# Mixture-of-experts outputs: one accumulating row pair per token in memory in place of eight separate rows per token

## The reference, cut to what matters

```
scores = sigmoid(h @ router_w)                  # 64 experts, 8 groups; each token gets 8 experts of 4 groups
gates  = 2.5 * scores of the chosen 8 / their sum
y      = sum over the 8 chosen e of (silu(h @ we_gate[e]) * (h @ we_up[e]) * gate_e) @ we_down[e]
shared = (silu(h @ ws_gate) * (h @ ws_up)) @ ws_down
x      = LN(alpha * x + (1 + gate2) * (y + shared))
```

## Time and profile before

| what | us |
|---|---|
| runs | 1685.2, 1704.44, 1702.05 (median 1702.05) |
| the profiled execution, by its own time | 1687.51 |
| its span, from the first to the last instruction | 1685.8 |
| TensorE busy | 1433.9 (85%) |
| VectorE busy | 581.6 (35%) |
| POOL busy | 243.8 (14%) |
| DMA moved | 318.40 MB, mean 189 GB/s |

### The profile page before, as it was taken

One profiled execution on the slowest core, in us unless ns is written; L12 is line 12 of the kernel. 1 busy time (PEld: TensorE's weight loads), 2 busy tenths in 40 slices (PEclk: granted clock), 3 DMA queues, 4 the chain that ended last, 5 costly groups with the idle time before them and its releaser, 6 DMA issues.

```text
span 1685.8 us, 21034 instructions
## 1 busy us (share of the span) xinstructions
PE 1433.9 (85%) x8007; PEld 927.3 (55%) x8007; DVE 581.6 (35%) x1400; ACT 262.7 (16%) x543; POOL 243.8 (14%) x281
## 2 busy tenths in 40 slices
PE   4889998686858988997897899898988888899966
PEld 1555554584637866965445465555555555555532
DVE  0423476456454324232245322222122212222217
ACT  2122432210011121211002111111111111111100
POOL 5000000030004102300000022222212121222210
PEclk7889899697879998999897899898888888898988
DMA  9365310201030020005414269999999999995444
GB/s 323 112 238 184 138 50 17 64 1 50 0 99 27 1 72 29 1 1 203 138 37 187 86 235 376 387 395 389 377 371 374 370 387 374 382 360 197 168 166 187
DMA packets 105489, 318.40 MB, mean 189 GB/s; under 512 B 22320, under 2 KB 39300, under 8 KB 88235
## 3 DMA queue, kind: packets, MB, share of 16 engines
q1 hardware_dynamic: 90694, 289.01, 46.4%
q0 software_dynamic: 12000, 25.20, 4.6%
q10 hardware_dynamic: 2692, 2.79, 0.5%
HBM read 304.53 MB, written 26.58 MB: 196 GB/s over the span
## 4 chain that ended last, share of the span: by engine, by line
PE 63%; DMA 22%; DVE 8%; SPq 3%; issue 2%; ACT 2%; POOL 0%; POOLq 0%; DVEq 0%; ACTq 0%
DMA ring<-in_we_up_dram 12%; PE bank L1924 11%; PE bank L1460 9%; DMA MT<-h_rows,slot_ids 6%; PE bank L1583 5%; PE bank L1934 4%; PE bank L1833 3%; PE bank L1801 3%; PE bank L1657 2%; DVE inv L872 2%; PE bank L1644 2%; PE bank L2022 2%; PE bank L1909 2%; PE bank L1654 2%; DVE ring L872 2%
## 5 line engine op out<-in xcount | busy, mean ns | idle before, releaser
L1924 PE MATMUL bank<-ring,MT 128*64 128x256 f32 x2400 | 338.3, 445 | 12.6 <-DMA ring<-in_we_up_dram 12.4
L1924 PEld LDWEIGHTS bank<-ring,MT 128*64 128x64 f32 x2400 | 194.2, 161 | 130.1 <-issue 54.5
L1347 DVE SCALAR_TENSOR_TENSOR gate<-zs,slot_gate,bank 128x128 f32<-128x128 f32 x75 | 26.1, 348 | 390.0 <-ACT zs L846 390.0
L1460 PE MATMUL bank<-hT,ring 128*128 128x384 f32 x416 | 145.5, 514 | 5.8 <-DVE hT L872 4.6
L426 POOL DMA_INDIRECT MT<-h_rows,slot_ids x75 | 71.4, 953 | 516.4 <-PE bank L1909 329.6
L1934 PE MATMUL bank<-inv,rwp 128*64 128x512 f32 x600 | 141.5, 593 | 0.4 <-ACT rwp L848 0.4
L1909 PE MATMUL bank<-ident,MT 64*128 64x64 f32 x600 | 82.8, 285 | 44.0 <-DMA MT<-h_rows,slot_ids 44.0
L1460 PEld LDWEIGHTS bank<-hT,ring 128*128 128x128 f32 x416 | 83.4, 202 | 65.6 <-issue 10.2
L1583 PE MATMUL bank<-hT,ring 128*128 128x384 f32 x256 | 89.9, 511 | 10.3 <-DMA ring<-in_w_in_dram 10.3
L1909 PEld LDWEIGHTS bank<-ident,MT 64*128 64x128 f32 x600 | 71.8, 200 | 47.6 <-DMA MT<-h_rows,slot_ids 46.6
L1583 PEld LDWEIGHTS bank<-hT,ring 128*128 128x128 f32 x256 | 50.6, 201 | 44.3 <-DMA ring<-in_w_in_dram 10.4
(11 more groups left out here) (364 smaller groups left out, 1836.8 us busy)
## 6 DMA issues: line engine op xcount, KB each, us to landing
ring<-in_we_gate_dram SPq DMA_DIRECT2D x64, 1024.0 KB, 10.5
ring<-in_we_up_dram SPq DMA_DIRECT2D x64, 1024.0 KB, 18.7
inv<-in_we_down_dram SPq DMA_DIRECT2D x64, 1024.0 KB, 13.5
ring<-in_w_ada_dram SPq DMA_DIRECT2D x12, 2048.0 KB, 14.6
ring<-in_w_in_dram SPq DMA_DIRECT2D x7, 2048.0 KB, 9.1
ring<-y_rows SPq DMA_DIRECT2D x6, 2048.0 KB, 8.6
ring<-in_w_in_dram SPq DMA_DIRECT2D x9, 1024.0 KB, 5.3
xs<-in_x_prompt_dram SPq DMA_DIRECT2D x2, 1024.0 KB, 16.9
```

What stands on the lines that cost most here:

```text
L1460: last = mm(bank[4 + n % 4][:, 0:T], ring[:, u, k, tok(c)], hT[:, k, :], start=(k == 0), stop=(k == KC - 1))
L1924: last = mm(b[HS * g:HS * g + HS, 0:DE].rearrange("p (w n) -> p w n", w=2), hgT[:, buf, k, :], gu_ring[:, slot, :, k, tok(g)], start=(k == ...
```

## The change

The scatters add to `y_sum`, an array in memory with one row (two half rows) per token, and every addend of a token goes to the same place. So a scatter now waits for the one before it, and the first waits for the shared expert's rows, which ScalarE's queue stores into `y_sum`. At the end the three tiles of `y_sum` are loaded (512 KB each) and go straight into `layernorm`; TensorE has no part in the end. In the routing the scan is gone and column 1 of `slot_rows` is the token's own row. Core of the diff (the same change of the indirect DMA is made in the second pass, where VectorE also moves the slots that a first task has done out of reach; that branch is left out here):

```diff
-        y_rows = nc.dram_tensor("y_rows", [2 * T * N_ACT, D // 2], F32).ap()
+        y_sum = nc.dram_tensor("y_sum", [2 * T, D // 2], F32).ap()
...
             def scatter(n):
                 pool.wait_ge(S("r_o"), n + 1)
+                if n == 0:
+                    pool.wait_ge(S("y_first"), 16 * TILES)
+                else:
+                    pool.wait_ge(S(f"r_sc{(n - 1) % 2}"), 16 * (even_odd(n - 1) + 1))
                 mark()
-                pool.indirect_dma_start(y_rows, bass.IndirectOffsetOnAxis(slot_ids[:, n % IDS, 1:2], 0),
-                                        obuf[n % 2], None, bounds_check=2 * N_ACT * T - 1, oob_is_err=False
-                                        ).then_inc(S(f"r_sc{n % 2}"), 16)
+                pool.indirect_dma_start(y_sum, bass.IndirectOffsetOnAxis(slot_ids[:, n % IDS, 1:2], 0),
+                                        obuf[n % 2], None, bounds_check=2 * T - 1, oob_is_err=False,
+                                        compute_op=ALU.add).then_inc(S(f"r_sc{n % 2}"), 16)
...
             sp_.wait_ge(S("routed"), 1)
-            y_v = y_rows.rearrange("(t p j a) d -> t p j (a d)", p=P, j=N_ACT, a=2)
-            for j in range(2 * TILES):
-                if j >= 3:
-                    sp_.wait_ge(S("ys_mm"), j - 2)
-                if j == 4:
-                    sp_.wait_ge(S("y_used"), 1)
-                load(y_in[:, j % 3], y_v[j // 2][:, 4 * (j % 2):4 * (j % 2) + 4, :], f"ring{j % 3}")
+            y_v = y_sum.rearrange("(t p a) d -> t p (a d)", p=P, a=2)
+            for t in range(TILES):
+                load(y_in[:, t, :], y_v[t], f"ring{t}")
...
+            act.wait_ge(S("y_sh"), 6)
+            y_v = y_sum.rearrange("(t p a) d -> t p (a d)", p=P, a=2)
+            for t in range(TILES):
+                load(y_v[t], y_sh[:, t, :], "y_first")
...
-                st.do(V.tensor_tensor_scan(tmp, ones[:, 0:NE], m, 0.0, ALU.mult, ALU.add))
-                ts(slot_rows[:, t, :, 1], tmp, 2.0, tok_id[:, t, 1:2], ALU.mult, ALU.add)
+                ts(slot_rows[:, t, :, 1], m, 0.0, tok_id[:, t, 1:2], ALU.mult, ALU.add)
...
-            dve.wait_ge(S("y_sh"), 6)
             for t in range(TILES):
-                j = 2 * t + 1
-                dve.wait_ge(S(f"ring{j % 3}"), 16 * (RING_END[j % 3] + j // 3 + 1))
-                rest = y_in[:, j % 3, 2, :]
-                tt(rest, rest, y_in[:, j % 3, 3, :], ALU.add)
-                dve.wait_ge(S("ys_mm"), j + 1)
-                layernorm(t, [bank[2 * t][:, :], bank[2 * t + 1][:, :]], 1, "y_ready", rest)
+                dve.wait_ge(S(f"ring{t}"), 16 * (RING_END[t] + 1))
+                layernorm(t, [y_in[:, t, 512 * j:512 * j + 512] for j in range(2)], 1, "y_ready")
...
-            pe.wait_ge(S("routed"), 1)
-            pe.wait_ge(S("y_sh"), 6)
-            for j in range(2 * TILES):
-                t, rows = j // 2, range(4 - 2 * (j % 2))
-                pe.wait_ge(S(f"ring{j % 3}"), 16 * (RING_END[j % 3] + j // 3 + 1))
-                for i in range(2):
-                    half = slice(512 * i, 512 * i + 512)
-                    if j % 2 == 0:
-                        mm(bank[2 * t + i][:, :], ident[:, :], y_sh[:, t, half], start=True, stop=False)
-                    for k in rows:
-                        last = mm(bank[2 * t + i][:, :], ident[:, :], y_in[:, j % 3, k, half],
-                                  start=False, stop=(j % 2 == 1 and k == rows[-1]))
-                sig(last, "ys_mm")
```

More of the change, by code:

```diff
@@ L226, in hybrid_kernel @@
         y_sh = flat(F13, 3 * D).rearrange("p (t n) -> p t n", t=TILES)
[L227 removed]
+        y_in = flat(ring, 3 * D).rearrange("p (t n) -> p t n", t=TILES)
         bank = [ctx.enter_context(nc.psum_tensor(f"bank{i}", [P, 512], F32)) for i in range(8)]
@@ L461, in _ @@
                         mark()
-                        pool.indirect_dma_start(y_rows, bass.IndirectOffsetOnAxis(slot_ids[:, 0, 1:2], 0),
-                                                obuf[0], None, bounds_check=2 * N_ACT * T - 1, oob_is_err=False
-                                                ).then_inc(S("r_sc0"), 16)
+                        pool.indirect_dma_start(y_sum, bass.IndirectOffsetOnAxis(slot_ids[:, 0, 1:2], 0),
+                                                obuf[0], None, bounds_check=2 * T - 1, oob_is_err=False,
+                                                compute_op=ALU.add).then_inc(S("r_sc0"), 16)
                 pool.wait_ge(S("r_sc0"), 16 * (EVEN + NE * REST))
@@ L1214, in _, with layernorm @@
                 tt(merged[:, c, :], mtmp[:, 0], mtmp[:, 1], ALU.add, "merged")
-            def layernorm(t, src_banks, which, name, rest=None):
+            def layernorm(t, src_banks, which, name):
                 kind = int(t == 2)
@@ L1222, in layernorm @@
                     src = src_banks[j]
-                    if rest is not None:
-                        tt(lt[:, half], src, rest[:, half], ALU.add, "y_used" if j else None)
-                        src = lt[:, half]
                     tt(lt[:, half], src, ga_tok[which][:, kind, 512 * j:512 * j + 512],
@@ L1359, in _ @@
                 dve.wait_ge(S("r_sc1"), 16 * ODD)
+                st.do(V.memset(load_key[:, 0:TWICE_FIRST], BIG), "late")
+                ts(load_key, load_key, key8[:, TWICE_LAST - 1:TWICE_LAST], -float(T), ALU.is_ge, ALU.mult, "late")
+                for t in range(TILES):
+                    ts(key_cmp, pos[:, t, :], float(P - 1), None, ALU.is_le, name="late")
+                    tt(key_cmp, key_cmp, load_key, ALU.mult, "late")
+                    tt(pos[:, t, :], pos[:, t, :], key_cmp, ALU.add, "late")
                 with dve.Fori(0, NE) as i:
```

3 lines of the change are left out of this document (1 added, 2 removed).

## The result

The changed kernel takes 1736.04 us (median of 4 runs, 1722.62 to 1740.02) where the kernel before takes 1698.82 (4 runs, 1685.2 to 1704.44): ratio **1.0231**, 95% interval 1.0196 to 1.0266: slower by 37 us between the medians, clear of noise, though the interval doesn't tell whether it is by more or by less than 2%. The forecast was 1705 us with no change as the likeliest case; 1736 lies within the range of 1668 to 1800, and at the very edge between the forecast's own range (to 1736) and its first rival, the scatter chain.

The account below looks back on a forecast made before the run. Weight bytes on full DMA engines bound the second regime, landing gathers the first. Loop and tail +30.0 less the end's 26.9 gave +3.1 us, forecast as 1705 us, no change; own range 1676 to 1736, 8 in 10 from 1668 to 1800.

Parts of the forecast that it names:

- the scatter chain: Rival: POOL's wait for the scatter before paces the loop, 1010 to 1480 us; from x = 1.7, +34; 1779 us at 2.5; chance 0.36.
- The end: After the routed loop: 59.3 us becomes 32.4 with 512 KB tiles going straight into layernorm, a gain of 26.9 us.
- The front: Before the loop: dropped scan, three more DMA issues on ScalarE and the first scatter's new wait change nothing.
- The restart: On POOL in the loop: time from a scatter's landing to the next scatter's start, taken as 0.85 us.
- Packets: In an adding scatter every half row becomes its own packet: 3.1 more turns per engine, 1.1 us.
- x, the later landing: Extra landing time of a scatter because it adds; taken as 1.1 us, bounds 0 and 8.1.
- The second regime: Loop from 1120 to 1480 us, DMA engines full: 38 tasks at 10.05 us against 9.47, +22.0 us.
- The floor of 23 us: Second regime: the adds' second read needs at most 23 us of full engines; a floor, not a further term.
- The credit of 8 us for slip: In the loop: a scatter can slip before it holds a gather up; 8 us taken off the loop's cost.
- The tail: Last scatters of the loop: 4.25 us apart for 2.56, and the last lands 1.1 later; +2.8 us.
- The addition is hidden: Rival: x under 0.5, scatters fit beside the loop and only the end counts; 1675 us; chance 0.17.
- The signs: End 32 us, add landings 8.8 to 9.8, POOL's waits naming the scatter before; wrong if POOL's instruction or gathers' landings grow.

Follow-up runs that it names:

- light kernels: Kernel before and changed kernel, each loading a quarter of every expert's weights to empty the DMA engines: 1574.03 and 1549.09 us.
- whole rows: Changed kernel, wait and one array kept, scattering 64 rows of 4 KB, not 128 of 2 KB: 1708.0 us, ratio 1.0074; again 1712.03 us.
- two-sums kernel: Changed kernel without the wait on POOL, even and odd tasks adding to two arrays that the end sums: 1704.0 us, ratio 1.0053.

## Why the prediction was right or wrong

In short: the mechanism that the prediction put first for a loss, a loop paced by landing plus restart, is the one that ran; its size in the second regime was less than half of what was measured, and with it the forecast of no change failed. What came is the first rival, at the very point where the prediction had it begin.

- **The end**: right. 32.4 us forecast, 32.6 measured; the landing of 512 KB was taken as 3.5 and is 3.62.
- **The front**: right, nothing to be seen. Of the first scatter's later start (12.3 us) 8.3 are there in a kernel with no change in that part too, and a changed kernel (with light weights) starts it 0.7 us later only.
- **The restart**: right. 0.85 taken; 0.76 read above for one scatter, and the median landing with 0.85, 9.8 + 0.85 = 10.65, meets the changed kernel's 10.67.
- **Packets**: right. Every half row is a packet of its own when it is added, 64 more per task, and taking them away again (whole rows) brings the landing down by 1.2 us, where the working had 1.1 for the turns. The agreement is in part luck: the working had counted the 50 rows with data, 3.1 on each engine, and the count rose by 64, the number of slots, 4.0 on each; and of the 1.2 us 0.15 may be POOL's instruction, which fell from 1.57 to 1.42.
- **x, the later landing**: mis-sized, 1.1 for 1.7 (9.8 less 8.1). The step had only the turns in it. Left out was POOL's own instruction, 1.57 us for 1.02, though the text named it among the signs of being wrong at the root. 1.05 to 1.2 for the turns and 0.55 of instruction would make 1.6 to 1.75; that the second part is that instruction is an inference from its length, as no run changed it alone.
- **The second regime, the term that failed**: +22.0 forecast, +52.2 measured. With x = 1.7 the working's own line gives 38 x 1.18 = 45. The rest is the line's unit: 40 tasks and not 38, and a base of 9.37 us and not 9.47. So what failed is the size of x in this term, not the wait that the term is about.
- **The floor of 23 us**: about right, and underrated. The two-sums kernel shows it: 21 us on POOL's queue, and 27.2 us of window without any wait on POOL, as the weights' packets took longer too. I used it as a floor under the wait's term only. It also means that no cure of the wait could have won more than 4 us against the end's 26.9, and by the measured 27.2 none at all, which I hadn't drawn from it. The rule of the Trainium skill ("Collectives: The Full Stack", section "The bandwidth ceiling: the fold count and why AG ≠ RS ≠ AR": in a ring's reduce step an add reads twice and runs at half the rate of a copy) is nearly met by the trace. Taking half of the 1.18 us per task for the scatters, an estimate, gives 0.59, and the adds took 0.53 more with half rows, 0.45 with whole ones.
- **The credit of 8 us for slip**: not seen. The first window lost 10.7 us where 13.2 − 8 had been forecast. The adds there land at 8.6 us (x = 0.7), so landing and restart ask for 9.45 us per task, and 115.16 / 12 = 9.60 were taken: nothing was slipped.
- **The tail**: +2.8 forecast. The last two scatters do stand further apart, 5.74 us for 2.56, but from scatter 57 to the last it is −2.2 us; the adds of this stretch cost nothing that can be seen.
- **The sum**: met by luck in part. At x = 1.7 the working's formula gives +34.6 us, and from the first scatter on the profiled executions differ by 34; but the second window cost 7 us more than its line, and the tail and the first window 8 us less.
- **The rivals**: "the scatter chain becomes the pace of the loop" is what happened, right at the point that was named for it (x = 1.7, +34; measured x = 1.7, and +37 between the medians). It had 0.36, the forecast 0.42. "The addition is hidden" is what the light kernels show.
- **The signs**: the end, the landings (9.8, at the edge of 8.8 to 9.8) and the period over 10.6 came. POOL's waits did not name the scatter before; the chain and VectorE's wait for the same landing show it. One sign of being wrong at the root came as well: the gathers land at 10.1 us behind the adds for 7.7. It wasn't the root, as gathers are 2.5% of the chain there; it goes away with the wait.

## What to carry to other kernels

An accumulating scatter is priced twice: as work on the DMA engines (here half a microsecond for some 50 rows of 4 KB), which is free where they have room and paid in full where they are the bound, and as a landing that has to be waited for, since the next add may name the same row. Before sums are moved into memory, compare the landing plus the restart with the period of the loop, and the second read with the share that the engines have left. Long rows take the extra packets away and, here, nearly all of the wait off the path; they don't take the work away.

## What the runs showed that I had not expected

- A plain indirect scatter of two neighbouring half rows of 2 KB seems to move them in one packet of 4 KB (6400 packets in the window, as many as the adding scatter of whole rows has); the adding one of half rows doesn't (8944).
- POOL's indirect instruction takes 1.02 us for 128 rows plain, 1.57 for 128 rows adding and 1.42 for 64 rows adding, so it goes with the add more than with the rows.
- The wait on every scatter's landing, alone, cost nothing within 0.3%, though it was on the chain at times.
